# One up panel of the first MLP streams its tokens in two halves

## The chip, the cores and the metric

The kernel runs on one core of one Trainium2 chip. The metric is the device time of one execution in microseconds, here the median of three runs.

## What is computed

The kernel computes one hybrid layer (a state-space mixer and sparse attention side by side, then an MLP) followed by one attention layer with a second MLP, for 256 tokens of width 2048, in float32. The change lies in the first MLP. Of the reference that is:

```python
D_MODEL, SEQ, D_FF = 2048, 256, 4 * 2048

x = x + jnp.concatenate([y_ssd, y_att], axis=-1) @ w_out
u = rmsnorm(x, g_mlp) @ w_up                      # [256, 2048] @ [2048, 8192]
return x + jnp.square(jax.nn.relu(u)) @ w_down    # [256, 8192] @ [8192, 2048]
```

The second layer's `sqrelu_mlp` has the same form.

## The kernel before

**Numbers in two parts.** Every large product is made with operands split into a high and a low part of type fp32r. A weight chunk lands in `raw`. ScalarE copies it, rounded, into `wh` (L648); VectorE writes `raw - wh` into `wl` (L1181). The tokens stand turned (features on the partitions) in `XHL`, one block of 128 features (a k tile) after another, each with 256 columns of the high part and 256 of the low part; `XH` and `XL` are its two halves. A product is high x high + high weight x low tokens + low weight x high tokens.

**Panels and chunks.** Weights are walked through in panels of 512 columns, a panel in four chunks of 1 MB. There are four slots for chunks in each of `raw`, `wh` and `wl`. SyncE issues the load of a chunk once the chunk four places earlier has been used up (`chunk_used`), ScalarE and VectorE split it (`hi`, `lo`), and TensorE waits for `lo_ready` ahead of each chunk. `chunk_used` is counted up by the last matmul of a chunk.

**The MLP.** The 8192 hidden columns are made in two halves of 4096. Each half has eight up panels (n = 0 to 7) and then its part of the down product. On TensorE panel 0 of the first half runs in `first_panel` with `k_tile` (L2115 to L2117: three matmuls of 256 columns each for a k tile and a block of 128 weights). All other up panels run in `half_cols` (L2089). There a chunk holds eight k tiles by 256 weight columns, and two chunks make a whole accumulation over 16 k tiles. For each k tile kk and each block f of 128 weight columns there are two matmuls, each with its own weight load:

- L2102: the high weight is loaded, and all 512 columns of `XHL[:, k]` are moved (256 high, then 256 low); the results go to the two halves of PSUM bank f.
- L2104: the low weight is loaded, and the 256 columns of `XH[:, k]` are moved; the result is added to the first half of the bank.

That gives 4 chunks x 8 k tiles x 2 blocks = 64 pairs a panel. After two chunks ScalarE copies the second half of each bank to `RB` (L768), VectorE adds the first half to it (L1352) and squares the positive part (L1357), ScalarE writes the high part `hh` (L774) and VectorE the low part `hl` (L1366). Two pairs of banks (`acc`) alternate; TensorE waits for a pair to come free (`acc_wait`) ahead of every second chunk.

**The order.** Each engine has its instructions written out by hand. On TensorE `mlp` (L2263) issues the panels of a half one after the other and then the down product. Nothing else of TensorE is issued among the up panels of this MLP. The other users of `half_cols` are the second half of this MLP, the second MLP and seven panels of the attention layer's projections.

Of the kernel before, what the change touches and what calls it, by code (L numbers as in the profile page):

```python
# [18 lines left out]
P = 128  # L19
TOK = 256  # L20
NT = TOK // P
D = 2048
KT = D // P
# [47 lines left out]
def hybrid_then_fox(nc, x, g_mix, w_in, conv_w, conv_b, dt_bias, a_log, d_skip, g_ssd, g_q, g_k,  # L71
# [3 lines left out]
    with ctx:  # L75
# [44 lines left out]
        def mixtures(start, at):  # L120
# [7 lines left out]
        X, XHL, wh = T["X"], T["XHL"], T["wh"]  # L128
        TH, TS, TL = ([T[n + at] for at in "01"] for n in ("TH", "TS", "TL"))
        XH, XL = XHL[:, :, 0, :], XHL[:, :, 1, :]  # L130
        arena = lined_up(region(arena, [("raw", slots, F32)], [("wl", slots, F32R)]))
        raw, wl = T["raw"], T["wl"]
        at = region(arena, [("SM", [P, NT, W_SMALL], F32), ("VB", [P, 3 * HEADS_S + HD_I], F32),
                            ("PR", [PARAMS + 3 * KT, P], F32), ("PC", [P, PARAMS], F32),
                            ("SQS", [P, 96], F32), ("DTS", [P, 10, NT * HEADS_S], F32),
                            ("FMm", [P, 3 * P], F32), ("Um", [P, P], F32), ("Vm", [P, P], F32),
                            ("MK", [P, 3 * P], F32), ("CB", [P, NT * GROUPS, P], F32),
                            ("BM", [P, NT, GROUPS * STATE], F32), ("Y", [P, NT, SSD_W], F32),
                            ("XD", [P, NT, SSD_W], F32)])
# [8 lines left out]
        at = region(at3, [("RCm", [P, TOK], F32), ("SMT", [W_SMALL, TOK], F32)], [("XDD", [P, SSD_W], F32)],  # L148
                    [("ST", [P, GROUPS, 512], F32)])

        at = region(at, [("U", [P, CONV_CH // P, TAPS - 1 + TOK], F32)],
                    [("Q", [P, NT, HEADS_A * HD], F32), ("K", [P, NT, KV_A * HD], F32)],
                    [("Z", [P, NT, SSD_W], F32)])
# [10 lines left out]
        at = region(arena, [("HB", [P, NT, D], F32)], [("FQ", [P, HEADS_F, TOK], F32)])  # L164
# [130 lines left out]
        def up_acc(half, n):  # L295

            return 2 * n - (1 if half == 0 and n else 0)
# [27 lines left out]
        def slot(buffer, b, j):  # L325


            high, low = PHASES.get((b, j), PHASES.get(b, (0, 0)))
            at = j * SLOT + ASIDE * (high if buffer is wh else low)
            return buffer[:, at:at + 4 * 512].rearrange("p (k n) -> p k n", n=512)  # L330
# [230 lines left out]
        def split(b, j):  # L561

            return 4 * b + j - 3
# [1495 lines left out]
        def _(pe):  # L2059
            def acc_wait(o, n=None):  # L2060

                n = o // 2 if n is None else n
                if not (isinstance(n, int) and n == 0):
                    for t in range(2):
                        pe.wait_ge(acc_freed[o % 2][t], n)
# [15 lines left out]
            def cols(b, j, o_par, first, last, k0):  # L2081
# [4 lines left out]
                    mm = k_tile(b, j, kk, o_par, first and kk == 0, last and kk == 3, k0 + kk)  # L2086
                mm.then_inc(chunk_used, 1)

            def half_cols(b, o):  # L2089

                for j in range(4):
                    x, e = o + j // 2, j % 2
                    if e == 0:
                        acc_wait(x)
                    pe.wait_ge(lo_ready, split(b, j))
                    for kk in range(8):
                        k = 8 * e + kk
                        at = 256 * (kk % 2)
                        for f in range(2):
                            bk = acc[x % 2][f]  # L2100
                            sh, sl = (slot(z, b, j)[:, kk // 2, at + f * P:at + (f + 1) * P] for z in (wh, wl))
                            pe.matmul(bk[:, :].rearrange("p (s t) -> p s t", s=2), sh, XHL[:, k, :, :],  # L2102
                                      start=k == 0, stop=False, skip_group_check=True)
                            mm = pe.matmul(bk[:, 0:TOK], sl, XH[:, k, :], start=False, stop=k == KT - 1,  # L2104
                                           skip_group_check=True)
                    mm.then_inc(chunk_used, 1)
                    yield j
# [58 lines left out]
            def first_panel(form, m, b, o, plan={}):  # L2166

                for j in range(4):
                    if j == 0:
                        acc_wait(o)  # L2170

                    wait_emptied(pe, ("xt", m, 2 * j))
                    wait_emptied(pe, ("xt", m, 2 * j + 1))
                    form(b, j, o % 2, j == 0, j == 3, 4 * j)
                    if j == 1:
                        turn_quarter(m, 3)
                    side_work(plan, j)
# [85 lines left out]
            def mlp(m, b0, o0, u0):  # L2263
                for half in range(2):
                    b, o, u = b0 + half * B_HALF, o0 + half * O_HALF, u0 + half * U_HALF[0]
                    for n in range(UP):
                        if half == 0 and n == 0 and m == 3:
                            normed_panel(m, b, o)
                        elif half == 0 and n == 0:
                            first_panel(cols, m, b, o)  # L2270
                        else:
                            for j in half_cols(b + n, o + up_acc(half, n)):
                                pass
                    if half:
                        for s in range(SLOTS):
                            pe.wait_ge(hl_ready, 2 * (u + s) + 2)
                            if s == UNITS[0]:
                                acc_wait(o + O_DOWN[1])
                                acc_wait(o + O_DOWN[1] + 1)
                            if s in UNITS:  # L2280
                                seven(m, b + UP, s, o + O_DOWN[1])
                            else:
                                eight(b + UP, s)
                    for n in range(2 * half, DOWN):
                        on = o + O_DOWN[half] + n
                        acc_wait(on)
                        for j in range(8):
                            if n == 0:

                                pe.wait_ge(hl_ready, 2 * (u + up_acc(half, j + 1)) + 2)  # L2290
                            if m == 3 and half == 1 and n == DOWN - 1 and j > 5:
                                continue
                            rows(b + UP + 2 * n + j // 4, j % 4, on % 2, j == 0, j == 7, 4 * j, hh, hl)
                            if half == 1 and m == 1 and j in ((3, 5) if n == 2 else (3,)):
                                turn_quarter(2, (n - 2) * 2 + j // 2 - 1)
                if m == 3:

                    rows(B_END - 1, 2, on % 2, False, False, 24, hh, hl, [0], None)
                    rows(B_END - 1, 3, on % 2, False, True, 28, hh, hl, [0], first_tokens)
                    rows(B_END - 1, 2, on % 2, False, False, 24, hh, hl, [1])  # L2300
                    rows(B_END - 1, 3, on % 2, False, True, 28, hh, hl, [1])
# [250 lines left out]
```

## Time and profile before

| | us |
|---|---|
| median of 3 runs | 2194.67 |
| lowest, highest | 2193.94, 2195.92 |
| the profiled execution's own time | 2193.99 |
| its span in the trace | 2192.3 |

The profile is of one execution. PE is TensorE's matmuls, PEld its weight loads, which overlap the matmuls, DVE is VectorE, ACT ScalarE, POOL GpSimd, SP SyncE. A matmul's recorded length is its whole passage through the engine, with an end that is modelled; matmuls overlap one another, so what one costs is read from the distance between starts. In a table of stretches "x" is the number of instructions that touch the stretch, and the clock is the share of TensorE's full speed that was granted. In the chain that ended last a piece is attributed from end to end, so pieces there do add up.

### The profile page before, as it was taken

The page shows a single profiled execution, that of the slowest core. Times are in us where ns is not written, and L with a number is a line of the kernel's source. Part 1 is how long each engine was busy: PE and PEld are TensorE (multiplying, and loading weights), DVE is VectorE, ACT ScalarE, POOL GpSimd, SP SyncE. Part 2 cuts the span into 40 slices and gives each one's busy share as a digit, 9 for nine tenths or more (in the row PEclk, how much of TensorE's full clock was granted, in tenths as well). Part 3 has the DMA queues.
Part 4 walks back from the last instruction along what each step waited for, and adds up shares of the span by engine and source line. Part 5 has one row for each costly group of instructions (what it writes and reads, how often), then busy time and mean ns, then how long its engine had stood idle before and what let it go on. Part 6 is the DMA issues. An engine that isn't in the chain of part 4 may idle for free.

```text
span 2192.3 us, 27623 instructions
## 1 busy us (share of the span) xinstructions
PE 2177.2 (99%) x11804; PEld 1880.4 (86%) x11804; DVE 1314.5 (60%) x1546; ACT 990.6 (45%) x1120; POOL 26.4 (1%) x71
## 2 busy tenths in 40 slices
PE   9999999999999999999999999999999999999998
PEld 9988788988888888888898888889888888888887
DVE  5788664566644466677455654546665444667764
ACT  6453563444433344444444444544445333445442
POOL 1000000000000000000001010000000000000000
PEclk9999999999999999999999999999999999999999
DMA  8455445566555666665566665555765556666674
GB/s 260 146 170 170 147 135 192 175 194 193 195 194 196 192 196 194 193 194 198 185 194 202 188 188 172 174 191 183 220 193 193 192 193 194 194 194 194 202 252 151
DMA packets 280985, 415.46 MB, mean 190 GB/s; under 512 B 13284, under 2 KB 167056, under 8 KB 280608
## 3 DMA queue, kind: packets, MB, share of 16 engines
q1 hardware_dynamic: 279376, 409.89, 58.3%
q0 software_dynamic: 1456, 3.81, 0.6%
q8 instruction: 93, 1.52, 0.3%
q14 instruction: 28, 0.23, 0.0%
q10 hardware_dynamic: 32, 0.01, 0.0%
HBM read 409.47 MB, written 4.21 MB: 189 GB/s over the span
## 4 chain that ended last, share of the span: by engine, by line
PE 96%; DVE 3%; ACT 0%; issue 0%; POOL 0%; DVEq 0%; POOLq 0%; ACTq 0%
PE bank L2102 25%; PE bank L2075 13%; PE bank L2077 13%; PE bank L2076 13%; PE bank L2104 12%; PE bank L2115 3%; PE bank L2117 3%; PE bank L2116 3%; PE bank L2222 3%; PE bank L2221 3%; PE bank L2223 3%; DVE wl L1181 1%; PE bank L2307 1%; PE bank L2163 1%; PE bank L2328 0%; PE bank L2337 0%
## 5 line engine op out<-in xcount | busy, mean ns | idle before, releaser
L1181 DVE TENSOR_TENSOR wl<-raw,wh 128x2048 fp32r<-128x2048 f32 x376 | 860.6, 2290 | 475.6 <-ACT wh L648 474.0
L648 ACT ACTIVATE wh<-raw 128x2048 fp32r<-128x2048 f32 x376 | 721.2, 1919 | 510.7 <-DMA raw<-in_mlp_w_dram 165.0
L2102 PE MATMUL bank<-XHL,wh 128*128 128x512 f32 x2368 | 810.1, 390 | 0.0
L2104 PE MATMUL bank<-XHL,wl 128*128 128x256 f32 x2368 | 654.2, 276 | 0.0
L2102 PEld LDWEIGHTS bank<-XHL,wh 128*128 128x128 f32 x2368 | 444.5, 188 | 92.5 <-issue 0.2
L2104 PEld LDWEIGHTS bank<-XHL,wl 128*128 128x128 f32 x2368 | 444.5, 188 | 0.3
L2075 PE MATMUL bank<-wh,hh 128*128 128x512 f32 x768 | 299.0, 389 | 0.0
L2076 PE MATMUL bank<-wl,hh 128*128 128x512 f32 x768 | 298.8, 389 | 0.0
L2077 PE MATMUL bank<-wh,hl 128*128 128x512 f32 x768 | 298.8, 389 | 0.0
L2075 PE MATMUL bank<-wh,XHL 128*128 128x512 f32 x576 | 229.4, 398 | 0.7 <-DVE XHL L1189 0.7
L2077 PE MATMUL bank<-wh,XHL 128*128 128x512 f32 x576 | 224.6, 390 | 0.0
L2076 PE MATMUL bank<-wl,XHL 128*128 128x512 f32 x576 | 224.2, 389 | 0.0
L768 ACT ACTIVATE RB<-bank 128x256 f32<-128x256 f32 x120 | 39.6, 382 | 360.4 <-PE bank L2104 360.4
L1352 DVE TENSOR_TENSOR RB<-bank,RB 128x256 f32<-128x256 f32 x120 | 45.4, 420 | 213.7 <-ACT RB L768 213.7
L2077 PEld LDWEIGHTS bank<-wh,hl 128*128 128x128 f32 x768 | 144.1, 188 | 30.1
L2075 PEld LDWEIGHTS bank<-wh,hh 128*128 128x128 f32 x768 | 144.2, 188 | 29.8
L2076 PEld LDWEIGHTS bank<-wl,hh 128*128 128x128 f32 x768 | 144.2, 188 | 29.7
L2115 PE MATMUL bank<-XHL,wh 128*128 128x256 f32 x512 | 145.8, 285 | 2.3 <-DVE XHL L1215 1.2
L2116 PE MATMUL bank<-XHL,wh 128*128 128x256 f32 x512 | 142.8, 279 | 0.0
L2117 PE MATMUL bank<-XHL,wl 128*128 128x256 f32 x512 | 142.7, 279 | 0.0
L2077 PEld LDWEIGHTS bank<-wh,XHL 128*128 128x128 f32 x576 | 108.1, 188 | 23.1
L2075 PEld LDWEIGHTS bank<-wh,XHL 128*128 128x128 f32 x576 | 108.2, 188 | 22.9 <-DVE XHL L1189 1.0
(407 smaller groups left out, 1823.7 us busy)
## 6 DMA issues: line engine op xcount, KB each, us to landing
raw<-in_mlp_w_dram SPq DMA_DIRECT2D x128, 1024.0 KB, 5.3
raw<-in_w_up_dram SPq DMA_DIRECT2D x64, 1024.0 KB, 5.3
raw<-in_w_down_dram SPq DMA_DIRECT2D x64, 1024.0 KB, 4.9
raw<-in_fox_w_in_dram SPq DMA_DIRECT2D x48, 1024.0 KB, 5.2
raw<-in_w_in_dram SPq DMA_DIRECT2D x40, 1024.0 KB, 5.0
raw<-in_w_out_dram SPq DMA_DIRECT2D x16, 1024.0 KB, 5.0
raw<-in_fox_w_out_dram SPq DMA_DIRECT2D x16, 1024.0 KB, 5.0
raw<-in_w_in_dram SPq DMA_DIRECT2D x16, 256.0 KB, 6.9
```

Source lines behind the costliest of these rows:

```text
L648: act.activation(slot(wh, b, j), slot(raw, b, j), ACT.Copy).then_inc(hi_ready, 1)
L1181: dve.tensor_tensor(slot(wl, b, j), slot(raw, b, j), slot(wh, b, j).bitcast(F32), ALU.subtract)\
L2075: pe.matmul(o, sh, mh, start=first and kk == 0, stop=False)
L2076: pe.matmul(o, sh, ml, start=False, stop=False)
L2077: mm = pe.matmul(o, sl, mh, start=False, stop=last and kk == 3)
L2102: pe.matmul(bk[:, :].rearrange("p (s t) -> p s t", s=2), sh, XHL[:, k, :, :], start=k == 0, stop=False, skip_group_check=True)
L2104: mm = pe.matmul(bk[:, 0:TOK], sl, XH[:, k, :], start=False, stop=k == KT - 1, skip_group_check=True)
L2115: pe.matmul(o, sh, mh, start=first and f % 2 == 0, stop=False, skip_group_check=True)
L2116: pe.matmul(o, sh, ml, start=False, stop=False, skip_group_check=True)
L2117: mm = pe.matmul(o, sl, mh, start=False, stop=last, skip_group_check=True)
L2221: pe.matmul(bk[:, :], a[0], w[0], start=first, stop=False)
L2222: pe.matmul(bk[:, :], a[0], w[1], start=False, stop=False)
```

## The change

A new routine `token_cols` is used for one panel: n = 5 in the first half of the first MLP (m = 1). It walks the same chunks, k tiles and blocks in the same order with the same waits and the same `chunk_used` increments. Inside a block it goes through the tokens in two halves of 128. For each half t it moves, under the high weight, 128 high and 128 low columns (256 in all, to two pieces of 128 columns in the bank's two halves), and then, under the low weight, the same 128 high columns. High and low weight are loaded anew for the second half. Where a block had two matmuls of 512 and 256 columns with two weight loads, it has four of 256, 128, 256 and 128 columns with four loads. The first matmul of all into a bank alone carries the start flag. All other panels stay as they are.

```diff
--- before.py
+++ after.py
@@ -2086,6 +2086,27 @@
                     mm = k_tile(b, j, kk, o_par, first and kk == 0, last and kk == 3, k0 + kk)
                 mm.then_inc(chunk_used, 1)
 
+            def token_cols(b, o):
+
+                for j in range(4):
+                    x, e = o + j // 2, j % 2
+                    if e == 0:
+                        acc_wait(x)
+                    pe.wait_ge(lo_ready, split(b, j))
+                    for kk in range(8):
+                        k = 8 * e + kk
+                        at = 256 * (kk % 2)
+                        for f in range(2):
+                            bk = acc[x % 2][f][:, :].rearrange("p (s t) -> p s t", s=2)
+                            sh, sl = (slot(z, b, j)[:, kk // 2, at + f * P:at + (f + 1) * P] for z in (wh, wl))
+                            for t in range(NT):
+                                here = slice(t * P, (t + 1) * P)
+                                pe.matmul(bk[:, :, here], sh, XHL[:, k, :, here], start=k == 0 and t == 0,
+                                          stop=False, skip_group_check=True)
+                                mm = pe.matmul(bk[:, 0, here], sl, XH[:, k, here], start=False, stop=k == KT - 1,
+                                               skip_group_check=True)
+                    mm.then_inc(chunk_used, 1)
+
             def half_cols(b, o):
 
                 for j in range(4):
@@ -2268,6 +2289,8 @@
                             normed_panel(m, b, o)
                         elif half == 0 and n == 0:
                             first_panel(cols, m, b, o)
+                        elif m == 1 and half == 0 and n == 5:
+                            token_cols(b + n, o + up_acc(half, n))
                         else:
                             for j in half_cols(b + n, o + up_acc(half, n)):
                                 pass
```

## Rows read from the trace of the kernel before

**Rows 1.** The page: busy time (share of the span) and instructions, 40 slices.

```profile
PE 2177.2 (99%) x11804; PEld 1880.4 (86%) x11804; DVE 1314.5 (60%) x1546; ACT 990.6 (45%) x1120; POOL 26.4 (1%) x71
...
PE   9999999999999999999999999999999999999998
...
PEclk9999999999999999999999999999999999999999
```

**Rows 2.** The page: the chain that ended last, by engine and by line.

```profile
PE 96%; DVE 3%; ACT 0%; issue 0%; POOL 0%; DVEq 0%; POOLq 0%; ACTq 0%
PE bank L2102 25%; PE bank L2075 13%; PE bank L2077 13%; PE bank L2076 13%; PE bank L2104 12%; PE bank L2115 3%; PE bank L2117 3%; PE bank L2116 3%; PE bank L2222 3%; PE bank L2221 3%; PE bank L2223 3%; DVE wl L1181 1%; PE bank L2307 1%; PE bank L2163 1%; PE bank L2328 0%; PE bank L2337 0%
```

**Rows 3.** TensorE's waits: engine, line, releaser: us in total, times, longest.

```profile
PE bank L2123 <- POOL ident L585: 2.3, 1, 2.3
...
PE bank L2115 <- DVE XHL L1891: 0.2, 1, 0.2
```

**Rows 4.** The page: groups L2102 and L2104: count, busy, mean ns, idle before.

```profile
L2102 PE MATMUL bank<-XHL,wh 128*128 128x512 f32 x2368 | 810.1, 390 | 0.0
L2104 PE MATMUL bank<-XHL,wl 128*128 128x256 f32 x2368 | 654.2, 276 | 0.0
```

**Rows 5.** Timeline of matmuls, 425.3 to 427 (start us, length us, what).

```profile
425.67 0.39 PE L2102 MATMUL bank<-XHL,wh 128*128 128x512 f32 x1
```

**Rows 6.** Panels 1 and 5: stretch, length, busy of each engine, clock, DMA.

```profile
425.67:447.64 21.97, 21.97 (x130) 19.37 (x129) 13.59 (x14) 10.63 (x12) 0.00 (x0) 1.00 0.62 192
...
512.92:534.68 21.76, 21.76 (x130) 19.25 (x129) 13.18 (x16) 9.79 (x12) 0.00 (x0) 1.00 0.62 194
```

**Rows 7.** Timeline of matmuls at the start of panel 5.

```profile
512.92 0.39 PE L2102 MATMUL bank<-XHL,wh 128*128 128x512 f32 x1
513.15 0.28 PE L2104 MATMUL bank<-XHL,wl 128*128 128x256 f32 x1
513.26 0.39 PE L2102 MATMUL bank<-XHL,wh 128*128 128x512 f32 x1
```

**Rows 8.** Timeline of weight loads at the same place.

```profile
512.81 0.19 PEld L2102 LDWEIGHTS bank<-XHL,wh 128*128 128x128 f32 x1
512.93 0.19 PEld L2104 LDWEIGHTS bank<-XHL,wl 128*128 128x128 f32 x1
```

**Rows 9.** Weight loads by shape: count, busy, mean ns, idle before.

```profile
L2104 PEld LDWEIGHTS bank<-XHL,wl 128*128 128x128 f32 x2368 | 444.5, 188 | 0.3
...
L2369 PEld LDWEIGHTS bank<-XHL,NHm 128*96 128x96 f32 x16 | 2.6, 161 | 0.0
...
L2364 PEld LDWEIGHTS bank<-XHL,NPf 128*32 128x32 f32 x16 | 1.7, 108 | 0.3
L2366 PEld LDWEIGHTS bank<-XHL,NPf 128*16 128x16 f32 x16 | 1.5, 94 | 0.1
```

**Rows 10.** The chain in order of time, 205.3 to 209.9.

```profile
206.06 3.52 PE bank L2433 x32
```

**Rows 11.** The chain in order of time, 1289.3 to 1292.

```profile
1289.61 0.66 PE bank L2307 x4
```

**Rows 12.** The chain in order of time, 1031.8 to 1033.2.

```profile
1032.10 0.87 PE bank L2163 x8
```

**Rows 13.** Timeline of weight loads, 209.2 to 209.8.

```profile
209.36 0.19 PEld L2075 LDWEIGHTS bank<-wh,XHL 128*128 128x128 f32 x1
209.47 0.19 PEld L2076 LDWEIGHTS bank<-wl,XHL 128*128 128x128 f32 x1
```

**Rows 14.** Panel 0 of this MLP, chunks 0 and 1 (96 matmuls and one).

```profile
401.64:412.86 11.22, 11.22 (x97) 11.21 (x96) 5.88 (x4) 3.26 (x5) 0.00 (x0) 1.00 0.60 188
```

**Rows 15.** Timeline of VectorE and ScalarE, 512.9 to 519.

```profile
513.61 0.76 DVE L1352 TENSOR_TENSOR RB<-bank,RB 128x256 f32<-128x256 f32 x2 [3.69 <-ACT RB L768]
...
513.12 0.66 ACT L768 ACTIVATE RB<-bank 128x256 f32<-128x256 f32 x2 [6.00 <-PE bank L2104]
```

## The prediction, made before the changed kernel had run

> **What bounds the kernel now.** I read five views, in this order. First the page's busy times and its slices [rows 1]: TensorE matmuls are busy 2177.2 us of a span of 2192.3 us, no slice of the forty falls below eight tenths, and the granted clock is at nine tenths or more everywhere. VectorE has 1314.5 us and ScalarE 990.6 us, so both have air. Then the chain that ended last [rows 2]: 96% of it is TensorE, and the line of the wide matmul in the routine that the change copies, L2102, carries a quarter. Then the list of TensorE's waits [rows 3]: ten waits, 6.9 us in all, the longest 2.3 us, the first and the last shown, and none is on L2102 or L2104, the two lines of the panel that is changed: their groups on the page have 0.0 us of idle time before them in 2368 instructions each [rows 4]. A microsecond added to TensorE in that panel is therefore a microsecond of the span; one saved there would be saved as well, as long as nothing else becomes late.
>
> Last I cut the panel itself out. The changed panel is n = 5 of the first half of the first MLP. The first of the seven half-column panels (n = 1 to 7) starts at 425.67 us [rows 5]; it lasts 21.97 us, to 447.64, and the ones behind it 21.76 us each (panel 5 stands for them) [rows 6], so that n = 5 begins at 447.64 + 3 x 21.76 = 512.92 and ends at 534.68. In it TensorE is busy all 21.76 us at a clock of 1.00, while VectorE has 13.18 us and ScalarE 9.79 us [rows 6] (its 130 matmuls in the row are its 128 and two still running out from the panel before). The panel is 64 pairs (four chunks, eight k tiles, two blocks of 128 weights), so a pair takes 21.76 / 64 = 340 ns. Its timeline [rows 7] says how this is divided: the 512-column matmul starts, the 256-column one starts 0.23 us later, the next pair 0.11 us after that. From the 340 ns, in the proportion of 512 to 256 columns, the steps are 226.7 and 113.3 ns, that is 0.443 ns a column. The recorded length of one matmul (0.39 and 0.28 us) is its whole passage and overlaps the next one; only the distance between starts counts.
>
> **What the change removes and adds.** Each pair becomes two pairs. Removed: 64 wide matmuls of 512 columns with their weight loads, 64 of 256 columns with theirs. Added: 128 of 256 columns with the high weight, 128 of 128 columns with the low weight, each with its own load, since high and low weights alternate and the count of loads equals the count of matmuls on the page [rows 1]. Columns moved are the same: 64 x 768 = 49152, and at 0.443 ns a column 21.76 us. So by columns alone the edit is free. What is added is 128 loads and 128 matmul starts. No wait, no DMA, no PSUM bank and no VectorE or ScalarE instruction is added or moved; the semaphore increments stay at the end of each chunk.
>
> **The price of a step.** The loads of the panel now [rows 8]: a load starts as the matmul before it starts (the load of 512.93 beside the matmul of 512.92), so it runs beside one matmul, the one whose step it must fit into. A step costs the longer of the moving columns and the next load. For the 256-column step the cover is 113.3 ns, and it is enough today. For the 128-column step the cover would be 128 x 0.443 = 56.7 ns. Is that enough for a load of 128 columns?
>
> Two sets of rows answer. The recorded length of an fp32r load falls with its width: 188 ns at 128 weight columns, 161 at 96, 108 at 32, 94 at 16 [rows 9]. That is (188 - 94) / 112 = 0.84 ns a column above a fixed passage, so 128 columns hold the load path for 128 x 0.84 = 107 ns. The second set is a stretch with short moving operands: 32 matmuls of 64 columns, full 128-column weights, take 3.52 us in the chain [rows 10], 110 ns each. Those are plain fp32; two fp32 matmuls of 128 and two of 256 columns take 0.66 us [rows 11], 0.66 / 768 = 0.86 ns a column, so 64 columns need only 55 ns. Their moving time is thus just that of my 128-column step, and the step still took 110 ns. Eight transposes with 128 columns take 0.87 us, 109 each [rows 12]. Behind the 64-column stretch two fp32r loads stand at 209.36 and 209.47, 0.11 us apart with almost nothing left to move between them [rows 13]: the load of this kernel's own weight type has the same period. I take 110 ns for the 128-column step, the row nearest to it in moving time and in weight size. Its bounds: 107 ns from below, if the slope is the truth; from above 117 to 118 ns, since steps of 256 columns with the same loads do take 11.22 / 96 = 117 ns in the first panel of this MLP [rows 14], where three loads in a row each have only a 256-column cover. The 256-column step I leave at 113.3 ns, with the same upper bound of 118.
>
> Sum: a new pair of steps is 113.3 + 110 = 223.3 ns, two of them 446.6, against 340 now: 106.6 ns more, times 64 is 6.8 us. With 107 for the short step: 2 x 220.3 - 340 = 100.6 ns, 6.4 us. If loads could be queued as deep as one likes, two loads of 109 still take 218 ns a pair, 96 ns more, 6.1 us. With 118 for all steps: 2 x 236 - 340 = 132 ns, 8.4 us.
>
> At this place a rule of the Trainium skill speaks against me. The page "TensorE: Matmul & The Clock Gate", section "Back-to-back issue gap", gives a sustained 81 ns a matmul at 128 columns and 131 ns at 512, loads included. The row for 512 columns here is 227 ns, so the trace does not agree with that pair of figures; the same page of the Trainium skill says, under "Weight-path perf modes", that the fast weight load is not used for FP32, which may be the reason.
>
> **What lies beside it and what is late next.** Nothing hides the 6.8 us, because TensorE has no idle time in this stretch. The instructions queued behind it on TensorE (panels 6 and 7, then the down product) shift as a block. ScalarE and VectorE follow TensorE: VectorE stands 3.69 us idle until ScalarE's copy of the accumulator, and ScalarE 6.00 us until the matmuls [rows 15]. SyncE's loads of the next weights wait for the same chunk counter. All three get up to 1.7 us more per chunk (6.8 / 4), so weights are ready earlier relative to their use, and nothing new becomes late. The pace afterwards is TensorE's again, so nothing of the loss is given back: the waits that could absorb it are not in the part behind, where the list [rows 3] has only short ones tied to norms that move along. Writing each PSUM bank in two pieces of 128 columns costs nothing by itself that the trace could show; no row shows such a piecewise write, and I bound it between 0 and the 118 ns of the upper case.
>
> The profiled execution took 2193.99 us for a span of 2192.3, the median of the three runs is 2194.67. So I expect a span of 2199.1 us, an own time of the profiled execution of 2200.8 and a median of 2194.67 + 6.8 = 2201.5 us.
>
> **The rivals.**
> 1. Loads collide as in the first panel. The steps become 117 to 118 ns, loss 8.4 us, time 2203.1. For it: the 117 ns row [rows 14]. Against: in the panel as it is, the high weight's load fits into the 256-column step at 113.3 ns, in all 64 pairs.
> 2. The load is hidden after all (this is the one that ends on the other side: not slower). The mechanism: the fp32r load is shorter than its record or overlaps two steps, so the short step stays at 56.7 ns and the panel at 21.76 us: 2194.7. It decides once a load holds its path for less than 57 ns. Against it: the slope [rows 9] and the 0.11 us between two fp32r loads [rows 13]. For it: no fp32r matmul under 256 columns stands in the trace, so its step is not seen there.
> 3. The load is partly hidden: the short step lies between 57 and 110 ns, at the middle 83.5 ns. Then 2 x 196.8 - 340 = 53.6 ns, 3.4 us, 2198.1. The skill's 81 ns of the section named above would give 2 x 194.3 - 340 = 48.6 ns, 3.1 us, 2197.8 by an estimate from that page.
> 4. A short matmul isn't overlapped with its successor's load at all: the short step is 110 + 56.7 = 166.7 ns. Then 2 x 280 - 340 = 220 ns, 14.1 us, 2208.8. Against it: the 64-column matmuls have 55 ns of their own and still step at 110, not at 165 [rows 10].
> 5. The change makes the kernel faster. Fewer columns per matmul remove nothing that TensorE waits for; I see no mechanism and keep a small rest.
>
> **How the numbers follow.** Forecast (6.1 to 7.3 us, own range 2200.8 to 2202.0) 0.65; rival 1 0.18; rival 2 0.05; rival 3 0.05; rival 4 0.05; rival 5 0.02. The predicted time is the forecast's, 2201.5. A change of under 0.2% (4.4 us) is about what a measurement of this kernel can't tell from none; so rivals 2 and 3 are "same", 0.10, rival 5 "faster", 0.02, and the rest "slower", 0.88. For the range I take forecast and rival 1, 2200.8 to 2203.1, and add about 1 us on both sides, since three runs of one kernel lay between 2193.94 and 2195.92: 2199.8 to 2204.3.
>
> **What would show it.** Right: the panel starts at 512.92 and lasts 28.6 us (28.2 to 30.2); its 128-column steps are 110 ns and its 256-column steps 113; the page counts 11932 matmuls and as many loads (11804 + 128); the panel behind lasts 21.76 us again; the list of TensorE's waits doesn't change; the granted clock stays at 1.00. Loads in the new panel start 0.11 us apart without a gap. Wrong: the panel lasts 21.8 us (rival 2), about 25 us (rival 3) or 36 us (rival 4), or steps of 117 appear in it (rival 1). If the panel lasts 28.6 us and the time does not follow, the step that fails is that nothing later gives time back.

## The result, and the profile after

The changed kernel takes 2204.63 us (median of five executions, 2202.9 to 2205.3) against 2194.67 us: a ratio of 1.0044 with a 95% interval of 1.0033 to 1.0056, about 10 us or 0.44% slower. The forecast was 2201.5 with a range up to 2204.3: the sign and the main cause were right, the loss was half as large again as forecast.

The page of the changed kernel, its span, its busy times and its two largest matmul groups:

```profile
span 2202.9 us, 27879 instructions
...
PE 2187.2 (99%) x11932; PEld 1892.3 (86%) x11932; DVE 1314.1 (60%) x1546; ACT 990.4 (45%) x1120; POOL 26.3 (1%) x71
...
L2123 PE MATMUL bank<-XHL,wh 128*128 128x512 f32 x2304 | 789.7, 391 | 0.0
L2125 PE MATMUL bank<-XHL,wl 128*128 128x256 f32 x2304 | 637.4, 277 | 0.0
```

Against [rows 1], 128 more matmuls and as many more loads, no more idle time of TensorE in these groups, and VectorE and ScalarE unchanged. The groups of the old routine, now L2123 and L2125, have 64 instructions fewer each and still no idle time before them [rows 4]. The list of TensorE's waits has ten entries as before, and none of them belongs to the panel. One has grown: the wait for `XHL` of L1891 is 0.8 us instead of the 0.2 of [rows 3], but it ends at 7.5 us, long before the changed panel.

The stretches of panels 5, 6 and 7 in the changed kernel (columns as in [rows 6]):

```profile
512.78:542.22 29.44, 29.44 (x259) 29.44 (x258) 13.17 (x16) 9.75 (x12) 0.00 (x0) 1.00 0.46 143
542.22:564.62 22.40, 22.40 (x131) 19.70 (x130) 13.18 (x16) 9.78 (x12) 0.00 (x0) 1.00 0.60 189
564.62:587.02 22.40, 22.40 (x131) 19.70 (x130) 13.18 (x16) 9.77 (x12) 0.00 (x0) 1.00 0.60 188
```

Here the loss can be read off. Panel 5 takes 29.44 us instead of the 21.76 of [rows 6]: 7.68 us. But panels 6 and 7, whose instructions are the same as before, take 22.40 us each: 0.64 us more each, 1.28 in all, which no step of the forecast had. The third part lies behind the pause ahead of the second MLP's first panel (stretches of the changed kernel, then the same place of the kernel before):

```profile
1491.00:1497.00 6.00, 4.35 (x32) 3.67 (x31) 3.75 (x10) 2.97 (x8) 0.00 (x0) 1.00 0.95 334
1497.00:1500.50 3.50, 3.50 (x19) 3.50 (x18) 3.29 (x4) 3.09 (x2) 0.00 (x0) 0.52 0.00 0
```

```profile
1482.20:1488.20 6.00, 4.36 (x33) 3.67 (x32) 3.76 (x10) 3.01 (x8) 0.00 (x0) 1.00 0.94 330
1488.20:1491.70 3.50, 3.50 (x34) 3.50 (x33) 3.28 (x4) 3.50 (x4) 0.00 (x0) 1.00 0.00 0
```

In 1497.0 to 1500.5 the granted clock is 0.52 of full speed: TensorE ran at 1.2 GHz instead of 2.4. It had waited 1.23 us shortly before. The steps show it, here the matmuls of 256 columns on the timeline of the changed kernel, 0.11 us apart at first and then 0.21:

```profile
1496.34 0.38 PE L2136 MATMUL bank<-XHL,wh 128*128 128x256 f32 x1 [1.23 <-DVE XHL L1215]
1496.56 0.28 PE L2137 MATMUL bank<-XHL,wh 128*128 128x256 f32 x1
1496.67 0.29 PE L2138 MATMUL bank<-XHL,wl 128*128 128x256 f32 x1
...
1497.76 0.41 PE L2136 MATMUL bank<-XHL,wh 128*128 128x256 f32 x1
1497.97 0.41 PE L2137 MATMUL bank<-XHL,wh 128*128 128x256 f32 x1
1498.18 0.41 PE L2138 MATMUL bank<-XHL,wl 128*128 128x256 f32 x1
```

Compared at the ends of the chunks, the two profiles part as follows: 0.1 us less up to panel 5, 7.7 more in it, 1.3 in panels 6 and 7, 1.6 in the first chunk of the second MLP and 0.2 two chunks later; sum 10.6, the difference of the spans (2202.9 - 2192.3). From the end of panel 7 to the second MLP the distance stays constant within 0.1 us for over 900 us. So nothing is given back, as forecast.

The 0.1 and the 0.2 us have a story of their own. Long before the changed panel, in code that is the same in both kernels, 144 matmuls of 256 columns stand in a row. The kernel before, then the changed one:

```profile
40.16:56.57 16.41, 16.41 (x147) 16.41 (x146) 9.71 (x8) 8.83 (x8) 0.00 (x0) 1.00 0.67 222
```

```profile
39.32:56.37 17.05, 17.05 (x148) 17.05 (x147) 9.77 (x8) 8.82 (x8) 0.00 (x0) 1.00 0.63 211
```

That is 114 ns a step in one profile and 118 in the other. Of all sixteen profiles of this study, five have this stretch at the faster pace and eleven at the slower one, although no instruction ahead of it differs. Such a row keeps its pace as a rule: 113.3 or 117.8 ns in the mean behind its first steps. The 0.2 us of the second MLP are the same thing in 48 matmuls, and the 0.1 us are what is left of larger differences to both sides. These two paces will be needed below.

How the time is made up inside panel 5 is seen on the weight loads of the changed kernel (start, length, what):

```profile
520.03 0.19 PEld L2104 LDWEIGHTS bank<-XHL,wh 128*128 128x128 f32 x1
520.14 0.19 PEld L2106 LDWEIGHTS bank<-XHL,wl 128*128 128x128 f32 x1
520.26 0.19 PEld L2104 LDWEIGHTS bank<-XHL,wh 128*128 128x128 f32 x1
520.37 0.19 PEld L2106 LDWEIGHTS bank<-XHL,wl 128*128 128x128 f32 x1
520.49 0.19 PEld L2104 LDWEIGHTS bank<-XHL,wh 128*128 128x128 f32 x1
```

A high weight's load (L2104) starts beside the 128-column matmul and the next load follows 0.11 us later, although that matmul has only 57 ns of columns. The low weight's load (L2106) starts beside the 256-column matmul and the next one follows 0.11 to 0.12 us later. Over the whole panel the mean distances are 108.5 ns and 121.5 ns (each lies within 107 to 114 and 115 to 126). Together 230 ns, times 128 is 29.44 us.

### The profile page after: what moved, and what is told of

Read it like the earlier page. It is cut to its first block, busy times and chain, and to the rows that moved or that the text cites. A ratio compares the mean times of both kernels' runs of the same rounds, so it can differ in the third digit from the quotient of the medians.

```text
span 2202.9 us, 27879 instructions
## 1 busy us (share of the span) xinstructions
PE 2187.2 (99%) x11932; PEld 1892.3 (86%) x11932; DVE 1314.1 (60%) x1546; ACT 990.4 (45%) x1120; POOL 26.3 (1%) x71
## 4 chain that ended last, share of the span: by engine, by line
PE 96%; DVE 3%; ACT 0%; issue 0%; POOL 0%; DVEq 0%; POOLq 0%; ACTq 0%
PE bank L2123 24%; PE bank L2075 13%; PE bank L2077 13%; PE bank L2076 13%; PE bank L2125 12%; PE bank L2136 3%; PE bank L2138 3%; PE bank L2137 3%; PE bank L2244 3%; PE bank L2243 3%; PE bank L2242 3%; PE bank L2104 1%; DVE wl L1181 1%; PE bank L2330 1%; PE bank L2184 1%; PE bank L2351 0%
## 5 line engine op out<-in xcount | busy, mean ns | idle before, releaser
L2123 PE MATMUL bank<-XHL,wh 128*128 128x512 f32 x2304 | 789.7, 391 | 0.0
L2125 PE MATMUL bank<-XHL,wl 128*128 128x256 f32 x2304 | 637.4, 277 | 0.0
L2123 PEld LDWEIGHTS bank<-XHL,wh 128*128 128x128 f32 x2304 | 432.6, 188 | 90.8 <-issue 0.2
L2125 PEld LDWEIGHTS bank<-XHL,wl 128*128 128x128 f32 x2304 | 432.8, 188 | 0.3
L2138 PE MATMUL bank<-XHL,wl 128*128 128x256 f32 x512 | 143.6, 281 | 0.0
```

Of the source, the lines that this page charges most:

```text
L2138: mm = pe.matmul(o, sl, mh, start=False, stop=last, skip_group_check=True)
```

## Experiments

**Splitting only the high weight.** Three steps of 256 columns a block, one more load, no short step:

```diff
-                                mm = pe.matmul(bk[:, 0, here], sl, XH[:, k, here], start=False, stop=k == KT - 1,
-                                               skip_group_check=True)
+                            mm = pe.matmul(bk[:, 0, :], sl, XH[:, k, :], start=False, stop=k == KT - 1,
+                                           skip_group_check=True)
```

> In panel 5 only the high weight's matmul is split (256, 256, then one of 256 for the low weight): three steps a block, each with one weight load. Theory A (a step costs the longer of its columns and the next load, and what cost 230 ns a half block in the changed kernel is the load left exposed behind the 128-column step, with the 256-column step behind it a few ns longer): no load is exposed, 3 x 113.3 = 340 ns, the panel lasts 21.8 us and the time stays at that of the kernel before. Theory B (the 121.5 ns of the 256-column step belong to moving the tokens in two pieces): 2 x 121.5 + 113.3 = 356 ns, panel 22.8 us, 1.0 us over the kernel before. Theory C (three loads in a row against 256 columns collide, as in the first panel of this MLP): 3 x 117 = 351 ns, panel 22.5 us. Tail in panels 6 and 7: by theory A none (21.76 us each); a tail here would say that it doesn't need an exposed load.

Measured 2197.34 us against 2194.83, a ratio of 1.0013 (1.0003 to 1.0022). Its panels 5, 6 and 7:

```profile
512.74:535.35 22.61, 22.61 (x195) 22.61 (x194) 13.17 (x16) 9.75 (x12) 0.00 (x0) 1.00 0.61 186
535.35:557.75 22.40, 22.40 (x131) 19.71 (x130) 13.17 (x16) 9.77 (x12) 0.00 (x0) 1.00 0.60 188
557.75:580.15 22.40, 22.40 (x131) 19.71 (x130) 13.16 (x16) 9.77 (x12) 0.00 (x0) 1.00 0.59 188
```

Panel 5 takes 22.61 us: 0.85 more than before, and 6.8 less than the full change. So the short steps carry the change's cost, as theory A says, but the three steps of 256 columns take 117.8 ns here instead of 113.3, the number of theory C. Its reason, that three loads in a row collide when each has only 256 columns beside it, isn't borne out: in the kernel before the same kind of sequence runs at both paces (16.41 us for 144 steps above, 11.22 us for 96 in [rows 14]). And panels 6 and 7 are at 22.40 us with no exposed load anywhere: the tail doesn't need one.

**Splitting only the low weight.** 512 columns, then 128 and 128:

```diff
-                            for t in range(NT):
-                                here = slice(t * P, (t + 1) * P)
-                                pe.matmul(bk[:, :, here], sh, XHL[:, k, :, here], start=k == 0 and t == 0,
-                                          stop=False, skip_group_check=True)
+                            pe.matmul(bk[:, :, :], sh, XHL[:, k, :, :], start=k == 0,
+                                      stop=False, skip_group_check=True)
```

> In panel 5 only the low weight's matmul is split (512, then 128 and 128): three steps a block. Theory A: the loads beside both 128-column steps are exposed, 227 + 2 x 108.5 = 444 ns, with 4 to 8 ns more behind each exposed load up to 460: the panel lasts 28.4 to 29.4 us, nearly the whole cost of the change with one more load instead of two, so that the cost goes by the short steps and not by the count of loads. Rival (every added load costs the same): half of the change's 7.7 us, panel 25.6 us. Panels 6 and 7: as in the changed kernel, 22.3 to 22.5 us each, if exposed loads set the tail.

The stretch of panel 5:

```profile
513.52:542.48 28.96, 28.96 (x195) 26.26 (x193) 13.18 (x16) 9.76 (x12) 0.00 (x0) 1.00 0.48 145
```

28.96 us, 453 ns a block (one execution, 2203.73 us in all), inside theory A's range and far from the 25.6 of the rival. One added load costs 7.2 us here and 0.85 in the kernel above; two cost 7.7. What counts is whether the load stands beside a 128-column step. The distances between loads: 108.3 and 110.9 ns beside the two short matmuls, 234 beside the 512 columns, which take 227 in the kernel before [rows 7]. Panels 6 and 7 take 22.60 us each, more than the 22.3 to 22.5 expected: 353 ns a pair, a pace slower still than the changed kernel's.

**Another order of the four.** 256, 256, 128, 128:

```diff
                                 pe.matmul(bk[:, :, here], sh, XHL[:, k, :, here], start=k == 0 and t == 0,
                                           stop=False, skip_group_check=True)
+                            for t in range(NT):
+                                here = slice(t * P, (t + 1) * P)
                                 mm = pe.matmul(bk[:, 0, here], sl, XH[:, k, here], start=False, stop=k == KT - 1,
```

> In panel 5 all four matmuls of a block stay, in the order 256, 256, 128, 128. Theory A: two loads exposed one behind the other, one 256-column step with a hidden load at 113.3 and one behind an exposed load at 121.5: 113.3 + 121.5 + 2 x 108.5 = 452 ns, panel 28.9 us against 29.4 with the alternating order. Rival (four loads at 115 ns each whatever the order): 460 ns, 29.4 us. Rival (the two 128-column steps share one 256-column cover, loads can be pulled ahead two deep): under 440 ns, 28.2 us. Tail in panels 6 and 7 as in the changed kernel.

The stretch of its panel 5:

```profile
513.12:542.50 29.38, 29.38 (x258) 29.38 (x257) 13.17 (x16) 9.77 (x12) 0.00 (x0) 1.00 0.46 144
```

29.38 us, 459 ns a block (one execution, 2203.81 us): the first rival's number, but not its mechanism, for the four loads don't take 115 ns each. The four distances are 122.7, 117.9, 108.6 and 110.8 ns. The exposed loads are as theory A has them; the 256-column step with a hidden load takes 117.9, not 113.3, and that makes the difference. The second rival, loads pulled ahead two deep, would have stayed under 440 ns. Panels 6 and 7 take 22.60 us each here too.

**The same change in panel 7, and in panel 2.**

```diff
-                        elif m == 1 and half == 0 and n == 5:
+                        elif m == 1 and half == 0 and n == 7:
```

> The change is made in panel 7 instead of 5, with the down product (512-column matmuls alone) right behind it. Panel 29.4 us, 7.7 us over. If the tail is a slower gait of the 512/256 steps that the changed panel leaves behind, nothing is there to be slowed: the down product keeps 226.7 ns a step and the loss is 7.7 us up to the first pause of the second MLP, against 9.0 in the changed kernel. Rival (the tail is a cost of its own that any stretch behind would pay): 1.3 us more also here.

The changed panel 7, and its successor in the chain in order of time (the down product, 512 columns a matmul):

```profile
556.16:585.60 29.44, 29.44 (x259) 29.44 (x258) 13.17 (x16) 9.75 (x12) 0.00 (x0) 1.00 0.43 144
```

```profile
586.22 0.23 PE bank L2077
586.45 0.23 PE bank L2075
586.68 0.23 PE bank L2076
```

2202.49 us against 2194.83, ratio 1.0035 (1.0022 to 1.0048). The panel takes the same 29.44 us, the down product keeps its 0.23 us a step, and at the end of the program the profile stands 7.4 us behind that of before. No tail, no stretch at half clock.

In panel 2 instead (n == 2 in the same line):

> The change is made in panel 2, with panels 3 to 7 behind it. Theory A (the changed panel leaves the 512/256 steps in a slower gait, 345 to 353 ns a pair instead of 340, and nothing in panels of the same kind ends it): five slow panels, 0.16 to 0.21 us a chunk, 3.2 to 4.2 us of tail and 10.9 to 11.9 us in all up to the down product. Rival (the tail is a disturbance that wears off after two panels, or hangs on the place of panel 5): 1.3 us of tail or none, 9 us in all.

Its stretches of panels 3 and 7 (4 to 6 take 22.40 us each as well):

```profile
476.82:499.20 22.38, 22.38 (x130) 19.68 (x129) 13.17 (x16) 9.77 (x12) 0.00 (x0) 1.00 0.63 189
...
566.40:588.80 22.40, 22.40 (x130) 19.70 (x129) 13.18 (x16) 9.77 (x12) 0.00 (x0) 1.00 0.58 188
```

Five panels behind it, five times 22.4 us against 21.76: 3.2 us of tail, and the slow gait (350 ns a pair instead of 340) ends only where the down product begins. It doesn't wear off in 320 pairs. The one execution took 2204.84 us against 2193.78 of the kernel before beside it, 11.1 us more, where 7.7 + 3.2 would be 10.9.

**Ending the gait.** Two ways. Two transposes of the identity ahead of panel 6:

```diff
                         acc_wait(x)
+                        if b == B_M1 + 6 and j == 0:
+                            warm(2, acc[x % 2][1])
```

> The changed kernel with two transposes of the identity put between panels 5 and 6 (into a free bank that the next matmul clears; 0.22 us of columns). If the gait is only a matter of when matmuls and loads start against each other, a short break in the sequence can end it: panels 6 and 7 at 21.76 us, 1.1 us less than the changed kernel. If it is set by where the operands lie in the memory, or comes back by itself, panels 6 and 7 keep 22.3 to 22.6 us. I hold the second for somewhat likelier, since the pauses and transposes elsewhere do not always end it.

Its stretches of panels 6 and 7:

```profile
542.63:564.60 21.97, 21.97 (x132) 19.52 (x132) 13.17 (x16) 9.78 (x12) 0.00 (x0) 1.00 0.63 192
564.60:586.40 21.80, 21.80 (x130) 19.35 (x129) 13.18 (x16) 9.78 (x12) 0.00 (x0) 1.00 0.59 194
```

Panel 6 takes 21.97 us with the transposes in it, panel 7 21.80: the tail is gone (one execution, 2202.21 us against 2193.78), against what I held for likelier. The second way moves only the place in memory of one chunk:

```diff
+        PHASES[B_M1 + 6, 0] = (1, 3)
```

> The changed kernel with the first chunk of panel 6 laid 0 and 192 bytes beside the usual place of high and low weights, as the first chunk of panel 1 is in the kernel before (high weights one step of 64 bytes, low weights three instead of none). There a chunk at 353 ns a pair was followed by 340 in all others. Theory: the change of place from chunk 0 to chunk 1 ends the slow gait: chunk 0 of panel 6 costs 0.2 us, the other seven chunks up to the down product nothing, so a tail of 0.2 to 0.3 us instead of 1.3. Rival (the place has nothing to do with it): the tail stays at 1.3 to 1.7 us.

Its stretches behind the changed panel:

```profile
542.63:548.25 5.62, 5.62 (x34) 4.92 (x33) 4.39 (x8) 4.88 (x6) 0.00 (x0) 1.00 0.64 190
548.25:564.56 16.31, 16.31 (x98) 14.46 (x97) 8.78 (x9) 4.89 (x6) 0.00 (x0) 1.00 0.62 194
564.57:586.30 21.73, 21.73 (x130) 19.28 (x129) 13.17 (x16) 9.77 (x12) 0.00 (x0) 1.00 0.61 194
```

The rows are chunk 0 of panel 6, its chunks 1 to 3 (16.31 us, three times 5.44), and panel 7. The tail is 0.2 us (one execution, 2202.32 us). In both runs the gait was slow in one stretch and fast behind a small disturbance, with the same instructions.

**Placing panel 5's weights elsewhere.** The low ones 128 bytes on, then the high ones instead:

```diff
+        PHASES[B_M1 + 5] = (1, 2)
```

> The changed kernel with the low weights of panel 5 laid 128 bytes further on (high ones unchanged). Theory (the 121.5 ns that the 256-column step takes in the changed panel instead of 113.3 come from the load of the low weight meeting the moving tokens in the memory): the step moves by several ns, the panel by 0.3 to 1 us either way, the exposed load behind the 128-column step stays at 108 to 109. Rival (the 8 ns are the price of starting behind an exposed load): 29.4 us unchanged. The tail behind may change in either case, since the last chunk leaves other places behind.

The stretch of its panel 5:

```profile
512.73:541.75 29.02, 29.02 (x259) 29.02 (x258) 13.17 (x16) 9.75 (x12) 0.00 (x0) 1.00 0.48 145
```

The panel drops from 29.44 to 29.02 us; the distance beside the 256 columns from 121.5 to 118.3 ns, the exposed one stays at 108.4. So part of the 8 ns is a matter of place. The tail behind is unchanged, 22.40 us a panel, and so it is in the next run (one execution each, 2202.51 and 2203.33 us).

```diff
+        PHASES[B_M1 + 5] = (3, 0)
```

> The changed kernel with the high weights of panel 5 laid 128 bytes further on (low ones unchanged). With the low ones moved the 256-column step had gone from 121.5 to 118.3 ns and the exposed load stayed at 108.4. Theory (the step depends on how the low weight's load meets the 256 moving columns; the high weight's load runs beside 128 columns and is exposed): the 256-column step stays at 121 to 122 and the panel at 29.4 us; at most the exposed step moves by 1 or 2 ns. Rival (any other distance between the two slots breaks the meeting): 118 ns and 29.0 us here too.

The stretch of its panel 5:

```profile
512.91:541.95 29.04, 29.04 (x259) 29.04 (x258) 13.18 (x16) 9.75 (x12) 0.00 (x0) 1.00 0.48 146
```

29.04 us, 118.4 and 108.4 ns: the same gain from moving the other weights. My theory that only the low weight's place counts has fallen; the rival, that another distance between the slots will do, holds for the two distances tried. The 5 ns that are left over 113.3 were not moved by any run; they are as large as the gap between the two paces of 256-column steps (113.3 and 117.8), but no run tells whether they are the same thing.

This run shows one thing more. A panel of the attention layer, 600 us behind the changed one and itself unchanged, takes 22.40 us here; in the run with the low weights moved it takes 21.78, as in the kernel before:

```profile
1132.31:1154.71 22.40, 22.40 (x131) 19.60 (x130) 12.57 (x11) 7.81 (x7) 0.00 (x0) 1.00 0.61 188
```

So the slow gait of the 512/256 sequence isn't bound to a changed panel right ahead of it. Among the sixteen profiles this is the only place where it came by itself.

**Does a nudge always help?** The kernel with only the high weight split, with two transposes ahead of panel 5 and two ahead of panel 6 (the line of the nudge above, in both routines):

> The kernel with only the high matmul of panel 5 split (256, 256, 256; its steps were 117.7 ns in the mean, panel 22.6 us), with two identity transposes ahead of panel 5 and two ahead of panel 6. Theory A (three steps of 256 columns bring the slow gait about themselves): panel 5 stays at 22.6 us plus 0.2 for the transposes, panel 6 and 7 come back to 21.76 us. Rival B (the slow gait is an accident of the start and holds until broken): panel 5 goes to 21.8 us plus 0.2.

Its stretches of panels 5, 6 and 7:

```profile
513.50:536.20 22.70, 22.70 (x195) 22.70 (x194) 13.18 (x16) 9.77 (x12) 0.00 (x0) 1.00 0.61 186
536.50:559.00 22.50, 22.50 (x130) 19.80 (x130) 13.18 (x16) 9.68 (x12) 0.00 (x0) 1.00 0.60 187
559.00:581.30 22.30, 22.30 (x129) 19.60 (x129) 13.18 (x16) 9.78 (x12) 0.00 (x0) 1.00 0.57 189
```

Panel 5 stays at 117.8 ns a step, as theory A has it; but that three 256-column steps always bring this pace about themselves is refuted by the 144 steps at 114 ns in the kernel before. And panels 6 and 7 stay slow too (22.50 with transposes, 22.30 in a stretch one matmul short), which neither theory had (one execution, 2197.19 us). So two transposes don't end the slow gait everywhere. It would fit that a disturbance draws the gait afresh, since rows of 256-column steps behind transposes come out at either pace, but for the 512/256 sequence that isn't shown.

**The stretch at half clock.** Ten transposes fill the pause ahead of the second MLP:

```diff
+                warm(10, acc[o % 2][1])
                 for k in range(KT):
                     if k == 0:
                         pe.wait_ge(norm_low, 1)
```

> The changed kernel with ten identity transposes (1.09 us) put into TensorE's pause of 1.23 us ahead of the first panel of the second MLP, behind which the changed kernel's profile has a stretch at half clock (granted 0.52 for 3.5 us, 1.6 us lost). Theory (the pause lets the clock fall in some executions, by where it lies in time): no stretch at half clock, panel 0 of the second MLP as in the kernel before; the time is that of the changed kernel's executions without the stretch, about 2203.0 against 2204.6, and spreads less. Rival (the transposes take the place of waiting but not of the work that the clock follows): the stretch still comes in some profiles. If the transposes reach past the pause the loss is under 0.3 us.

Its stretches around the filled pause and behind it:

```profile
1491.50:1497.50 6.00, 5.44 (x42) 4.76 (x41) 3.77 (x10) 2.97 (x8) 0.00 (x0) 1.00 0.95 330
1497.50:1501.00 3.50, 3.50 (x32) 3.50 (x31) 3.29 (x4) 3.50 (x4) 0.00 (x0) 1.00 0.03 10
```

2203.13 us (2202.96 to 2203.62), a ratio of 1.004 (1.0026 to 1.0054). The clock stays at 1.00 behind the filled pause, and the profile ends 9.1 us behind that of before: 7.7 + 1.3 and small change. The same in the kernel before:

> The same ten transposes in the kernel before, whose profile has no stretch at half clock. Theory: the median moves by less than 1 us, downwards if some of its executions have the stretch (they lie between 2193.9 and 2196.6), and the slow end of the spread goes. Rival: no difference at all, or 0.1 to 0.3 us more because the transposes end later than the pause.

2194.45 us against 2194.40, ratio 0.9998 (0.9989 to 1.0008). Its ten executions lie between 2193.57 and 2194.81; of the fourteen of the kernel before beside them three stood at 2195.65 to 2196.41. The mean granted clock recorded with each execution says more: it is 0.998 in the two slowest of them, 2196.41 and 2196.02, and 0.999 in the other twelve and in all fifteen with the pause filled, in either kernel.

The changed kernel once more, unchanged:

> The changed kernel once more. Its profile had 7.7 us in panel 5, 1.3 in panels 6 and 7 and 1.6 at half clock. Theory (the last is there in some executions and not in others): single executions fall into two groups, around 2203.2 and around 2204.8 us, and the group decides the median; the profile here has the panel at 29.4 us and panels 6 and 7 at 22.4, and shows the stretch at half clock behind the pause or does not, with its own time on the matching side of 2204. Rival (the stretch is a steady part of the changed kernel): all executions at 2204.5 to 2205.5, the profile with the stretch.

2204.19 us (2203.18 to 2205.31). The profiled execution took 2204.74 us and has the stretch again (the same stretches as above):

```profile
1491.00:1497.00 6.00, 4.36 (x32) 3.63 (x31) 3.72 (x10) 2.84 (x8) 0.00 (x0) 1.00 0.98 339
1497.00:1500.50 3.50, 3.50 (x20) 3.50 (x19) 3.29 (x4) 3.22 (x2) 0.00 (x0) 0.56 0.00 0
```

The five executions form no two clear groups by time (2203.18, 2203.84, 2204.19, 2204.74, 2205.31), so the rival of a steady stretch isn't borne out. Of the sixteen profiles of this study thirteen have the unfilled pause, 1.23 us in each of them, and the stretch stands in three of these: both of the changed kernel and that of the split high weight alone.

These three have a mean granted clock of 0.998, the thirteen other profiles 0.999, so the mean can serve as a mark for executions without a trace. It is a rough one: a stretch takes only 0.0008 off the mean, and rounding may hide one. Of the ten executions of the changed kernel five have the mark, at 2204.63 to 2205.31 us; the five without it lie at 2202.90 to 2204.47. The theory's two groups are there, then, but they nearly touch. Of the 38 executions of the kernel before whose clock was recorded, four have the mark, at 2195.57 to 2196.41, among its slowest; of the split high weight one of ten; of the other kernels with the pause left open none of thirteen; of those with the pause filled none of twenty. So the stretch comes in the kernel before too. It was seen more often in the changed kernel, but not in its close relatives, and what decides was not found.

And with both additions, the two transposes ahead of panel 6 and the ten in the pause:

> The changed kernel with both additions: two transposes between panels 5 and 6 and ten in the pause. If the loss has the three parts named, only the panel's 7.7 us and the 0.2 us of the two transposes are left: 7.9 us over the kernel before, about 2202.3 us, in a narrow spread of 1 us, panels 6 and 7 at 21.76 us. Rival (the two transposes draw the gait afresh and it can come out slow, as it did behind the split of the high weight alone): panels 6 and 7 stay at 22.4 us and the time at 2203.4.

Its stretches of panels 6 and 7:

```profile
542.53:564.50 21.97, 21.97 (x132) 19.51 (x132) 13.17 (x16) 9.79 (x12) 0.00 (x0) 1.00 0.61 192
564.50:586.26 21.76, 21.76 (x130) 19.30 (x129) 13.17 (x16) 9.78 (x12) 0.00 (x0) 1.00 0.61 194
```

2202.17 us (2201.64 to 2203.38), ratio 1.0033 (1.0021 to 1.0046): 7.5 us over the kernel before, where 7.9 was expected, with panels 6 and 7 fast. With tail and stretch taken away only the panel is left, within what the medians can tell.

## Why the prediction was right or wrong

**Right: the bound.** That TensorE has no idle time in the stretch, that nothing hides the loss, that columns alone cost nothing and that no other engine comes late: all four hold, in the panel's row, in the waits behind it and in the distance that stays constant for 900 us.

**Right: the short step.** 110 ns was taken from the 64-column matmuls [rows 10]; 108.5 was measured. The slope of the loads' recorded lengths [rows 9] gave 107. Rows with another element type and another line were good enough, because they had the same load and the same moving time. The transposes of [rows 12] were no support: by the prediction's own 0.86 ns a column, 128 plain fp32 columns need 110 ns whatever the load does. Rivals 2 and 3 (a load hidden, wholly or partly) and rival 4 fell with this, and rival 1 too: it had 117 to 118 ns for both steps and 8.4 us for the panel, of which 7.7 were measured. The 81 ns of the Trainium skill (page "TensorE: Matmul & The Clock Gate", section "Back-to-back issue gap") don't hold for this load: 108.5 was measured, and the trace decides.

**Wrong: the 256-column step.** "The 256-column step I leave at 113.3 ns" is the term that was mis-sized: 121.5. Times 128 that is 1.05 us, less 0.2 for the short step: the panel took 29.44 us instead of 28.6, still within the 28.2 to 30.2 given for it. The upper bound of 118 was too low as well. I had taken the step from a single sequence, in which every second load has the 227 ns of a 512-column matmul beside it, and the bound from [rows 14], read as three loads that collide. That reading was wrong: the trace of the kernel before has rows of such steps at 113 ns too, so what [rows 14] shows is the slower of two paces and not the price of three loads. Measured were 117.8 ns with no short step in the panel (the split high weight), and 118 to 123 behind an exposed load. Of the 8 ns 3 depend on the place of the weights; the cause of the rest is open.

**Wrong: "the panel behind lasts 21.76 us again".** This step failed, for 1.28 us. The forecast treated what stands behind as a block that shifts. Its rows held a warning that I didn't use: panel 1 took 21.97 us and panel 2 and the rest 21.76 with equal instructions [rows 6]. The difference lies in panel 1's first chunk, whose low weights stand in another place, the one that was later tried in panel 6. The runs in panels 2 and 7 show that the changed panel leaves a slower gait, 350 ns a pair instead of 340, that lasts until another kind of sequence begins; the two that ended it show that a small disturbance can be enough to go from one gait to the other. Why a sequence takes one gait or the other stays open.

**Wrong: "the granted clock stays at 1.00".** In the profiled execution 1.6 us. In the medians it weighs less: the changed kernel is 9.96 and 9.51 us over the kernel before measured beside it, with the pause filled 8.73, so 0.8 to 1.2 us, a difference that the intervals of the ratios don't resolve. By the recorded clocks five of ten executions of the changed kernel have the stretch, and four of 38 of the kernel before. That the change brings it can't be said: the panel's edit doesn't touch that place.

**The sum.** 6.8 forecast; 7.7 panel, 1.3 tail, and 1.6 clock in the profile, against 10.0 in the medians. The range ended 0.3 us below the median, since it took rival 1 inside the panel only and let nothing happen outside it.

No version here beats the kernel before. The change with both repairs is still 7.5 us slower, and the milder split of the high weight alone 2.5 us.

## What to carry to other kernels

Splitting the moving side of a matmul multiplies the weight loads: before doing it, divide the load's period (here 108 ns for 128 fp32r columns) by the time of a column (0.443 ns), about 245 columns, and keep every step above that. The 245 is an estimate from these two numbers; no width between 128 and 256 was run. A 128-column step costs nearly as much as a 256-column one (108.5 and 113.3 ns). Take the price of a step from several places of the trace before you rely on it: the same kind of step stood there at 113 and at 118 ns, and one stretch alone shows only one of the two. And when an edit on the bounding engine is timed, compare the unchanged code behind it too; a sequence can come out of it in another gait.

## What the hardware showed that I had not expected

- The same sequence of 512- and 256-column matmuls runs at 340 or 350 ns a pair (227 + 113 or 232 + 118), behind two of the variants at 353, and stays there for up to 5 panels and 320 pairs. Two identity transposes ended the slow gait behind the changed panel and not behind the split of the high weight alone.
- Rows of 256-column matmuls alone have two paces as well, 113.3 and 117.8 ns a step, and which one a row of 144 takes differs between profiles in code that is the same: five of sixteen had the faster one.
- A load beside 128 columns takes 108 to 111 ns in every order and place tried; the 256-column step behind it takes 118.3 to 122.7, and 3 ns of that hang on where the weights' slots lie.
- After a pause of 1.23 us in TensorE the granted clock fell to half for about 3.4 us in three of thirteen profiles, beginning 0.8 to 1.0 us after TensorE was back at work, at a cost of 1.6 us; in the ten others with the same pause it did not.
